# Short units' logits in a bank of their own, value products of two heads as column tiles, and moved steps at borders and in the state-space stage

## The chip, the core and the metric

The kernel runs on one core of one Trainium2 chip. The metric is device microseconds of one execution, as the median of three runs. The core's engines run side by side and meet only through semaphores: TensorE (PE in the profile, PEld for its weight loads), VectorE (DVE), ScalarE (ACT), GpSimd (POOL) and SyncE (SP), which here only issues loads. SBUF is the on-chip memory, PSUM the banks that TensorE writes.

## What is computed

Four layers on 256 tokens of width 1024, all float32: an "even" and an "odd" layer, then two hybrid layers. Each has a mixer and a gated convolution feed-forward part, each behind an RMS norm. The parts that the change touches, cut to what matters:

```python
# odd layer: dilated attention, 3 groups (window, dilation) x 4 heads of width 64
s = where(mask_g, q_g @ k_g.T, -inf)          # per head, 256 x 256, masks (128,1) (512,4) (2048,16)
m = max(s); p = exp(s - m); den = sum(p)
o = (p @ v_g) / den                           # lse = m + log(den)
out = sum_g softmax_g(lse) * o                # over the three groups
# hybrid layer: attention over the 64 best of 256 keys (8 heads of 128), beside a state-space scan
merged = sigmoid(g_attn) * (a @ w_proj_attn) + sigmoid(g_ssd) * (ssd @ w_proj_ssd)
# every norm
h = x * rsqrt(mean(x * x) + eps) * gain
```

Since the three groups share one softmax, the kernel masks the three groups' logits side by side in one row, takes one maximum, one exponential and one sum per row, and divides before the value product.

## The kernel before

Activations lie with channels on the 128 partitions and the 256 tokens along the free axis. Weights come as **slabs** of 2 halves, each 128 x 1024 (or 768, 512) float32. SP loads a slab into one of 3 slots (`w_raw`), ACT rounds it to fp32r (`w_hi`, line 1500), and POOL or DVE takes the remainder `w_lo = w_raw - w_hi` (`split_lo`, line 553). Each product is then three matmuls: hi by hi, hi by lo, lo by hi (`passes`, lines 784 to 786), or, in the feed-forward parts, a 512 wide one over the hi and lo operand side by side and a remainder (lines 805 and 809). ACT rounds 3 slabs ahead of the products, POOL and DVE split 2 slabs ahead: POOL half 0 and DVE half 1 in most stages. Results go to a ring of 4 PSUM banks `lin`; `logit`, `tr` and `stat` are PSUM too. Every engine works through its own program in the written order, so a wait holds up all that stands behind it on that engine.

**Dilated attention** (odd layer, once). 8 units u: head u // 2, token half t = u % 2. A short unit (t = 0) has 128 keys for each of 3 groups, a long one (t = 1) 256. The steps of a unit: `at_logits` on PE (line 1207, into `logit`), `at_mask` on DVE (scale and mask, line 2361, then the row maximum, line 2365), `at_exp` on ACT (line 1796), `at_probs` on DVE (reciprocal and scaling, lines 2373 and 2374), `at_transposes` on PE (line 1220, into `tr` and `stat`), `at_copy` on ACT (lines 1803 and 1805, to one of two buffers `pt1`), `at_values` on PE (line 1231: 3 or 6 matmuls of 64 output columns, into `lin`), `at_result` on ACT (line 1812). PE's program runs logits two units ahead of transposes, and values one behind; at_logits(u) waits until the mask of unit u - 1 has read the bank. Quarters of the first output slab (`late_part` of od_out[0]) stand between units. The four scans of the recurrence (line 2395), its gating (line 2399) and its rounding on ACT (line 1822) run at the same time. `v_copy(2)` (line 1789) empties the last slab of the values' projection, and PE waits for it (`stage_released`) before it goes on to unit 1.

**Borders.** A stage that adds to x (`residual` on ACT and POOL, `add_residual` on DVE) ends with four slabs j = 0 to 3, two channel chunks of x each. After each, ACT writes the gained x rounded and in float32 (line 1541), and its remainder `h_lo` is taken by POOL (chunks 0 to 3, line 562) or DVE (chunks 4 to 7). POOL's program: remainders of chunks 0, 1 after split j = 0, chunks 2, 3 after split j = 1, then split j = 2, a wait until DVE has taken all four of its remainders, and split j = 3. The first slabs of the next stage work on this not yet normalised h, and their results are scaled later; meanwhile `normalise` on DVE (lines 2023 to 2027) makes the normalised chunks in float32, ACT rounds them (`scaled`, line 1526) and POOL (4 chunks) and DVE (4 chunks) take the remainders `n_lo`. The up products of the two hybrid layers use them from slab 2 on; there PE waits first for all 8 rounded chunks, then chunk by chunk for the remainders. POOL splits both halves of the first slabs there, and `older_taps` on DVE (line 2143) runs the convolution.

**Hybrid layers** (twice). In the z stage, unit u of the sparse attention and two z slabs alternate; `by_token` (line 1348) transposes 4 chunks into `stat` and DVE copies them to SBUF (`stepped`, line 2599); the second transposes of a long unit (line 1374) need `stat` free. In the gates stage, DVE splits a slab's weights and then runs `ssd_out` (line 2650) for two chunks; PE's `group_cb` (line 1401) waits for it.

## Time and profile before

| what | value |
|---|---|
| median of 3 runs | 1689.92 us (1689.84 to 1690.18) |
| the profiled execution | 1691.72 us |
| its span | 1689.9 us |
| mean granted TensorE clock | 0.997 |
| PE busy | 1665.1 us, 99% |
| DVE busy | 1353.9 us, 80% |
| ACT busy | 1086.8 us, 64% |
| POOL busy | 754.0 us, 45% |
| DMA, mean of the 16 engines | about 50% |

"Busy" is the time in which at least one instruction of the engine was open. Matmuls overlap: a 256 wide fp32r matmul is open for 0.28 us, and the next one starts 0.12 us after it. A true float32 matmul is recorded as two instructions. "A <- B" means that A started when B had ended.

### The profile page before, as it was taken

The page shows a single profiled execution, that of the slowest core. Times are in us where ns is not written, and L with a number is a line of the kernel's source. Part 1 is how long each engine was busy: PE and PEld are TensorE (multiplying, and loading weights), DVE is VectorE, ACT ScalarE, POOL GpSimd, SP SyncE. Part 2 cuts the span into 40 slices and gives each one's busy share as a digit, 9 for nine tenths or more (in the row PEclk, how much of TensorE's full clock was granted, in tenths as well). Part 3 has the DMA queues.
Part 4 walks back from the last instruction along what each step waited for, and adds up shares of the span by engine and source line. Part 5 has one row for each costly group of instructions (what it writes and reads, how often), then busy time and mean ns, then how long its engine had stood idle before and what let it go on. Part 6 is the DMA issues. An engine that isn't in the chain of part 4 may idle for free. (4 is left out here: it accounts for less than half of the span.)

```text
span 1689.9 us, 28488 instructions
## 1 busy us (share of the span) xinstructions
PE 1665.1 (99%) x10944; PEld 1497.1 (89%) x10944; DVE 1353.9 (80%) x2174; ACT 1086.8 (64%) x1832; POOL 754.0 (45%) x454
## 2 busy tenths in 40 slices
PE   9999999999999999999999999999999999999997
PEld 8998889998888899999788988889999878888887
DVE  7978887494987878895996699778887699579795
ACT  7676576675775584776654676657467665378572
POOL 8631115962110367764554521048675465351113
PEclk9999999999999999999999999999999999999999
DMA  8545655541555555453345456556455335546552
GB/s 305 165 155 191 209 171 179 199 124 50 190 187 191 190 172 188 161 184 125 127 161 189 147 176 212 168 181 199 152 175 175 125 125 174 175 138 200 192 182 87
DMA packets 81239, 287.10 MB, mean 170 GB/s; under 512 B 9168, under 2 KB 9680, under 8 KB 80976
## 3 DMA queue, kind: packets, MB, share of 16 engines
q1 hardware_dynamic: 79776, 282.10, 50.4%
q10 hardware_dynamic: 1328, 3.18, 0.5%
q8 instruction: 87, 1.43, 0.3%
q14 instruction: 48, 0.39, 0.1%
HBM read 283.90 MB, written 1.05 MB: 169 GB/s over the span
## 5 line engine op out<-in xcount | busy, mean ns | idle before, releaser
L553 POOL TENSOR_TENSOR w_lo<-w_raw,w_hi 128x1024 fp32r<-128x1024 f32 (+2 forms) x239 | 570.2, 2405 | 308.7 <-ACT w_hi L1500 225.3
L1500 ACT ACTIVATE w_hi<-w_raw 128x1024 fp32r<-128x1024 f32 (+1 forms) x544 | 543.1, 1033 | 253.8 <-PE lin L786 162.7
L553 DVE TENSOR_TENSOR w_lo<-w_raw,w_hi 128x1024 fp32r<-128x1024 f32 (+1 forms) x305 | 456.7, 1502 | 31.0 <-ACT w_hi L1500 30.0
L784 PE MATMUL lin<-hid_pair,w_hi 128*128 128x256 f32 x1152 | 329.9, 286 | 1.8 <-POOL w_lo L553 1.7
L785 PE MATMUL lin<-hid_pair,w_hi 128*128 128x256 f32 x1152 | 326.1, 283 | 0.0
L786 PE MATMUL lin<-hid_pair,w_lo 128*128 128x256 f32 x1152 | 326.1, 283 | 0.0
L784 PEld LDWEIGHTS lin<-hid_pair,w_hi 128*128 128x128 f32 x1152 | 221.1, 192 | 6.3 <-issue 5.5
L785 PEld LDWEIGHTS lin<-hid_pair,w_hi 128*128 128x128 f32 x1152 | 221.2, 192 | 0.2
L786 PEld LDWEIGHTS lin<-hid_pair,w_lo 128*128 128x128 f32 x1152 | 221.2, 192 | 0.0
L562 POOL TENSOR_TENSOR hid_pair<-arena,hid_pair 128x256 fp32r<-128x256 f32 x64 | 53.3, 839 | 326.2 <-ACT std L1575 178.3
L805 PE MATMUL logit<-h_pair,w_hi 128*128 128x512 f32 x540 | 146.7, 392 | 0.0
L805 PE MATMUL lin<-h_pair,w_hi 128*128 128x512 f32 x540 | 136.2, 392 | 3.6 <-ACT h_pair L1526 1.7
L2143 DVE SCALAR_TENSOR_TENSOR acc<-arena,par,acc 128x254 f32<-128x254 f32 (+1 forms) x264 | 126.5, 521 | 7.6 <-ACT acc L1584 4.7
L805 PEld LDWEIGHTS lin<-h_pair,w_hi 128*128 128x128 f32 x540 | 101.0, 188 | 27.2 <-POOL h_pair L562 2.5
L805 PEld LDWEIGHTS logit<-h_pair,w_hi 128*128 128x128 f32 x540 | 97.1, 189 | 17.5
L784 PE MATMUL lin<-h_pair,w_hi 128*128 128x256 f32 x320 | 92.6, 289 | 2.1 <-POOL w_lo L553 1.4
L562 POOL TENSOR_TENSOR h_pair<-arena,h_pair 128x256 fp32r<-128x256 f32 x32 | 23.9, 757 | 152.1 <-ACT acc L1575 101.9
L785 PE MATMUL lin<-h_pair,w_hi 128*128 128x256 f32 x320 | 90.5, 283 | 0.0
L786 PE MATMUL lin<-h_pair,w_lo 128*128 128x256 f32 x320 | 90.5, 283 | 0.0
L805 PE MATMUL logit<-hid_pair,w_hi 128*128 128x512 f32 x324 | 89.1, 392 | 0.0
L784 PE MATMUL lin<-w_hi,hid_pair 128*128 128x512 f32 (+1 forms) x224 | 87.0, 388 | 0.0
L786 PE MATMUL lin<-w_hi,hid_pair 128*128 128x512 f32 (+1 forms) x224 | 84.0, 375 | 0.0
(407 smaller groups left out, 3581.6 us busy)
## 6 DMA issues: line engine op xcount, KB each, us to landing
w_raw<-in_upA SPq DMA_DIRECT2D x112, 512.0 KB, 4.5
w_raw<-in_upB SPq DMA_DIRECT2D x64, 512.0 KB, 4.6
w_raw<-in_xbc SPq DMA_DIRECT2D x48, 512.0 KB, 4.3
w_raw<-in_dnA SPq DMA_DIRECT2D x32, 512.0 KB, 4.5
w_raw<-in_dnB SPq DMA_DIRECT2D x32, 512.0 KB, 4.1
w_raw<-in_z SPq DMA_DIRECT2D x32, 512.0 KB, 4.4
w_raw<-in_gates SPq DMA_DIRECT2D x32, 512.0 KB, 4.4
w_raw<-in_ps SPq DMA_DIRECT2D x32, 512.0 KB, 4.0
```

Source lines behind the costliest of these rows:

```text
L553: eng.tensor_tensor(w_lo[slab.slot][:, half, part], w_raw[slab.slot][:, half, part], w_hi[slab.slot][:, half, part].bitcast(F32), ALU.subt ...
L562: return eng.tensor_tensor(lo, whole, hi.bitcast(F32), ALU.subtract)
L784: nc.tensor.matmul(out, lhs[0], rhs[0], start=first, stop=False)
L785: nc.tensor.matmul(out, lhs[0], rhs[1], start=False, stop=False)
L786: return nc.tensor.matmul(out, lhs[1], rhs[0], start=False, stop=last)
L805: return nc.tensor.matmul(outs[half], tile_of(slab, half, k)[0], pairs[k], start=(k == 0), stop=(half == 1 and k == last))
L1500: nc.scalar.activation(w_hi[slab.slot][:, half, part], w_raw[slab.slot][:, half, part], ACT.Copy)\
L2143: ins = stt(outs[i][:, d:T], ins_[i][:, 0:T - d], weight(taps - 1 - d, i), outs[i][:, d:T], ALU.mult, ALU.add)
```

## The change

It has seven parts.

1. **Logits.** Short units' logits go to the `lin` bank of od_out[1] (`at_early`), long units' stay in `logit`. at_logits(u) waits for the mask of unit u - 2, no longer of u - 1.
2. **Mask and maximum.** In the dilated and in the sparse attention, scaling, masking and the row extreme are one `tensor_tensor_reduce` (a negated sum and its minimum), which is emitted as the operation and a read of its accumulator. The exponential takes a scale of -1. The dilated one replaces two instructions by these two, the sparse one 4 + 1 by 4 x 2.
3. **Values.** Two heads' products with the same t form a pair and alternate matmul by matmul, one head in output columns 0 to 63, the other in 64 to 127, into one bank. They run after units 3, 4 and 7; `pt1` has 4 buffers instead of 2, and 4 result copies of 128 partitions replace 8 of 64.
4. **Border, POOL.** The split of j = 1 stands ahead of the remainders of chunks 0 and 1, and that of j = 2 ahead of those of chunks 2 and 3. The wait for DVE's last two remainders is gone; that for its first two stays.
5. **Normalised chunks.** POOL takes 3 remainders instead of 4, DVE 5; chunk 3 lies in `tr` in float32. The copy of the reciprocal root stands behind the remainders. In the hybrid layers' up products, PE waits for each rounded chunk as it comes to it. POOL holds back one split (slab 3, half 1) until the convolution taps of unit 0 are done.
6. **z stage.** The last by_token of u = 1 stands between the halves of its z slab.
7. **Gates stage.** At m = 3, DVE's weight split stands behind ssd_out.

PE in the dilated attention, before: unit 4's transposes, unit 3's values (6 matmuls), unit 7's logits. `lin` holds values here, `logit` logits.

```order
L1207 MATMUL logit<-arena 128x128 x3
L1220 MATMUL tr<-cst,arena 128x128 x3
L1231 MATMUL lin<-arena 64x128 x6
L1207 MATMUL logit<-arena 128x256 x3
L1220 MATMUL tr<-cst,arena 128x128 x4
L1220 MATMUL stat<-cst,arena 128x128 x2
L1231 MATMUL lin<-sq,arena 64x128 x3
```

The same place after:

```order
L1219 MATMUL lin<-arena 128x128 x3
L1232 MATMUL tr<-cst,arena 128x128 x3
L1246 MATMUL lin<-sq,arena 64x128 x12
L1219 MATMUL logit<-arena 128x256 x3
L1232 MATMUL tr<-cst,arena 128x128 x4
L1232 MATMUL stat<-cst,arena 128x128 x2
```

The 6 matmuls of unit 3 became 12 of units 1 and 3, the short unit's logits go to `lin`, and unit 4's values behind unit 5's transposes are gone from here.

POOL at the border before od_lru, before, with what each row waits for. `h_lo_v` counts DVE's remainders.

```order
L553 TENSOR_TENSOR w_lo<-w_raw,w_hi 128x768 [waits w_hi] x3
L562 TENSOR_TENSOR hid_pair<-arena,hid_pair 128x256 [waits h_f32,h_hi] x2
L553 TENSOR_TENSOR w_lo<-w_raw,w_hi 128x768 [waits w_hi]
L562 TENSOR_TENSOR hid_pair<-arena,hid_pair 128x256 [waits h_f32,h_hi] x2
L553 TENSOR_TENSOR w_lo<-w_raw,w_hi 128x1024 [waits w_hi]
L553 TENSOR_TENSOR w_lo<-w_raw,w_hi 128x1024 [waits w_hi,h_lo_v]
L553 TENSOR_TENSOR w_lo<-w_raw,w_hi 128x1024 [waits w_hi,w_lo1]
L553 TENSOR_TENSOR w_lo<-w_raw,w_hi 128x1024 [waits w_hi]
L562 TENSOR_TENSOR h_pair<-sq,h_pair 128x256 [waits n_f32,n_hi] x4
```

After:

```order
L565 TENSOR_TENSOR w_lo<-w_raw,w_hi 128x768 [waits w_hi] x4
L574 TENSOR_TENSOR hid_pair<-arena,hid_pair 128x256 [waits h_f32,h_hi] x2
L565 TENSOR_TENSOR w_lo<-w_raw,w_hi 128x1024 [waits w_hi]
L574 TENSOR_TENSOR hid_pair<-arena,hid_pair 128x256 [waits h_f32,h_hi] x2
L565 TENSOR_TENSOR w_lo<-w_raw,w_hi 128x1024 [waits w_hi,h_lo_v]
L565 TENSOR_TENSOR w_lo<-w_raw,w_hi 128x1024 [waits w_hi,w_lo1]
L565 TENSOR_TENSOR w_lo<-w_raw,w_hi 128x1024 [waits w_hi]
L574 TENSOR_TENSOR h_pair<-sq,h_pair 128x256 [waits n_f32,n_hi] x3
```

Each pair of remainders moved behind one more split, the last split's wait asks for two of DVE's remainders instead of four, and three normalised chunks are left to POOL.

The diff, cut to its core (declarations of the two semaphores that go are left out):

```diff
-            return sq[:, c, :] if c < DC // 2 else logit[:, c - DC // 2, :]
+            if c < NORM_POOL:
+                return sq[:, c, :]
+            return tr[:, T:2 * T] if c < DC // 2 else logit[:, c - DC // 2, :]
...
-        pt1 = (sqf[:, 0:6 * P], arena[:, 54 * T:57 * T])
+        pt1 = (arena[:, 54 * T:54 * T + 3 * P], sqf[:, 0:6 * P], arena[:, 54 * T + 3 * P:57 * T], sqf[:, 6 * P:12 * P])
...
         at_bank = [lin[slab_at("od_out", n).bank] for n in (2, 3)]
+        at_early = lin[slab_at("od_out", 1).bank][:, :, :].rearrange("p h t -> p (h t)")
+
+        def at_logit(t):
+
+            if t == 0:
+                return at_early[:, 0:DIL_G * P].rearrange("p (g k) -> p g k", g=DIL_G)
+            return logit[:, 0:DIL_G, :]
+
+        def at_pair_of(u):
+
+            return 2 * (u // 4) + u % 2
...
-                for c in range(DC // 2):
+                for c in range(NORM_POOL):
...
                 for k in range(COUNT[stage]):
                     j = k - (COUNT[stage] - 4)
-                    if j == 3 and n < 8:
-                        pool.wait_ge(s.h_lo_v, DC // 2 * n + 4)
                     split_lo(pool, slab_at(stage, k, l).ahead(SPLIT_AHEAD), 0)
-                    if j in (0, 1) and n < 8:
-                        norm_lo(n, (2 * j, 2 * j + 1))
+                    if j in (1, 2) and n < 8:
+                        norm_lo(n, (2 * j - 2, 2 * j - 1))
                     if j == 2 and n < 8:
                         pool.wait_ge(s.h_lo_v, DC // 2 * n + 2)
                     if j == 2 and n not in FOLDED:
...
                         for half in range(2):
+                            if k == 1 and half == 1:
+                                pool.wait_ge(s.ffn2_tap, 4 * l * FC + 4)
                             split_lo(pool, slab_at("upA" + sfx, k, l).ahead(SPLIT_AHEAD), half)
...
                 def wait_lo(k):
-                    half = DC // 2
-                    if k < half:
-                        pe.wait_ge(s.n_lo_p, half * number + k + 1)
+                    if k < NORM_POOL:
+                        pe.wait_ge(s.n_lo_p, NORM_POOL * number + k + 1)
                     else:
-                        pe.wait_ge(s.n_lo_v, half * number + k - half + 1)
+                        pe.wait_ge(s.n_lo_v, (DC - NORM_POOL) * number + k - NORM_POOL + 1)
...
                         def wait_chunk(c):
-                            if c == 0:
-                                wait_hi(KC - 1)
+                            wait_hi(c)
                             wait_lo(c)
...
             def at_logits(u):
                 head, t = u // 2, u % 2
                 lo = 64 * (head % 2)
-                if u >= 1:
-                    pe.wait_ge(s.at_masked, u)
+                if u == 0:
+                    slab_at("od_v", 0).wait_released(pe)
+                if u >= 2:
+                    pe.wait_ge(s.at_masked, u - 1)
                 for g in range(DIL_G):
                     c = (g * DIL_H + head) // 2
-                    mm = nc.tensor.matmul(logit[:, g, 0:(t + 1) * P], qn[lo:lo + 64, c, t * P:t * P + P],
+                    mm = nc.tensor.matmul(at_logit(t)[:, g, :], qn[lo:lo + 64, c, t * P:t * P + P],
                                           kn[lo:lo + 64, c, 0:(t + 1) * P], start=True, stop=True)
...
 
-            def at_values(u):
-                head, t = u // 2, u % 2
-                lo, nb = 64 * (head % 2), DIL_G * (t + 1)
-                pe.wait_ge(s.at_pt, u + 1)
-                if u >= 2:
-                    pe.wait_ge(s.at_out, u - 1)
+            def at_values(p):
+
+                units = (4 * (p // 2) + p % 2, 4 * (p // 2) + p % 2 + 2)
+                t, nb = p % 2, DIL_G * (p % 2 + 1)
+                pe.wait_ge(s.at_pt, units[1] + 1)
+                if p >= 2:
+                    pe.wait_ge(s.at_out, p - 1)
                 for b in range(nb):
-                    v_at = (b // (t + 1) * DIL_H + head) * DIL_D
-                    mm = nc.tensor.matmul(at_bank[u % 2][lo:lo + 64, 0, 0:P], vt[:, b % (t + 1), v_at:v_at + DIL_D],
-                                          pt1[u % 2][:, b * P:b * P + P], start=(b == 0), stop=(b == nb - 1))
+                    for u in units:
+                        head = u // 2
+                        lo, v_at = 64 * (head % 2), (b // (t + 1) * DIL_H + head) * DIL_D
+                        mm = nc.tensor.matmul(at_bank[p % 2][lo:lo + 64, 0, 0:P], vt[:, b % (t + 1), v_at:v_at + DIL_D],
+                                              pt1[u % 4][:, b * P:b * P + P], start=(b == 0), stop=(b == nb - 1))
                 mm.then_inc(s.at_pv, 1)
...
                     slab.wait_split(pe, half)
-            BESIDE = (2, 4, 6, 7)
+            BESIDE, VALUES_BEHIND = (2, 4, 6, 7), (3, 4, 7)
             for u in range(1, UNITS):
                 if u + 2 == 4:
                     slab_at("od_qk", 5).wait_released(pe)
@@ -1261,8 +1276,10 @@
                 if u + 2 < UNITS:
                     at_logits(u + 2)
                 at_transposes(u)
-                at_values(u - 1)
-            at_values(UNITS - 1)
+                if u in VALUES_BEHIND:
+                    at_values(VALUES_BEHIND.index(u))
+            at_values(3)
+            pe.wait_ge(s.at_masked, UNITS - 1)
...
+                    if u == 1:
+                        slab_products(slab_at("z", 2 * u + 1, l), operand, between=lambda: by_token(3))
+                    else:
+                        slab_products(slab_at("z", 2 * u + 1, l), operand)
+                        by_token(2 * u + 1)
 
                 pe.wait_ge(s.da_out, 4 * l + 4)
...
-                act.wait_ge(s.at_max, u + 1)
-                nc.scalar.activation(score[:, u % 2, 0:n], score[:, u % 2, 0:n], ACT.Exp,
+                act.wait_ge(s.at_masked, u + 1)
+                nc.scalar.activation(score[:, u % 2, 0:n], score[:, u % 2, 0:n], ACT.Exp, scale=-1.0,
                                      bias=small[:, 16 + u:17 + u], accum_out=small[:, 24 + u:25 + u]).then_inc(s.at_exp, 1)
 
...
                 n = DIL_G * (u % 2 + 1) * P
                 act.wait_ge(s.at_tr, u + 1)
+                if u >= 4:
+                    act.wait_ge(s.at_pv, at_pair_of(u - 4) + 1)
                 first = min(n, 4 * P)
-                ins = nc.scalar.activation(pt1[u % 2][:, 0:first], tr[:, 0:first], ACT.Copy)
+                ins = nc.scalar.activation(pt1[u % 4][:, 0:first], tr[:, 0:first], ACT.Copy)
                 if n > first:
-                    ins = nc.scalar.activation(pt1[u % 2][:, first:n], stat[:, T:T + n - first], ACT.Copy)
+                    ins = nc.scalar.activation(pt1[u % 4][:, first:n], stat[:, T:T + n - first], ACT.Copy)
                 ins.then_inc(s.at_pt, 1)
 
-            def at_result(u):
-                head, t = u // 2, u % 2
-                lo = 64 * (head % 2)
-                act.wait_ge(s.at_pv, u + 1)
-                nc.scalar.activation(acc[lo:lo + 64, 0, head // 2, t * P:t * P + P], at_bank[u % 2][lo:lo + 64, 0, 0:P],
-                                     ACT.Copy).then_inc(s.at_out, 1)
+            def at_result(p):
+                t = p % 2
+                act.wait_ge(s.at_pv, p + 1)
+                nc.scalar.activation(acc[:, 0, p // 2, t * P:t * P + P], at_bank[p % 2][:, 0, 0:P], ACT.Copy).then_inc(s.at_out, 1)
 
...
-                at_result(u - 1)
+                if u in (4, 5, 7):
+                    at_result((4, 5, 7).index(u))
                 if u + 2 < UNITS:
                     at_exp(u + 2)
-            at_result(UNITS - 1)
-            act.wait_ge(s.at_out, UNITS)
+            at_result(3)
+            act.wait_ge(s.at_out, 4)
             nc.scalar.activation(raw_set(1)[0][:, NC4:NC4 + 2, :], acc[:, 0, :, :], ACT.Copy).then_inc(s.att_hi, 1)
...
-                    act.wait_ge(s.da_max, 4 * l + u + 1)
+                    act.wait_ge(s.da_masked, 4 * l + u + 1)
                     for i in range(QPK):
-                        ins = nc.scalar.activation(da_score[u % 2][:, i, 0:n], da_score[u % 2][:, i, 0:n], ACT.Exp,
+                        ins = nc.scalar.activation(da_score[u % 2][:, i, 0:n], da_score[u % 2][:, i, 0:n], ACT.Exp, scale=-1.0,
...
+                for c in range(NORM_POOL, DC):
                     dve.wait_ge(s.n_hi, DC * number + (c | 1) + 1)
                     lo_part(nc.vector, lo[:, c, :], normed_f32(c), hi[:, c, :]).then_inc(s.n_lo_v, 1)
+                nc.vector.tensor_copy(std[:, 0, 0:T], rstd).then_inc(s.rstd_copied, 1)
                 dve.wait_ge(s.rstd_copied, number + 1)
-                dve.wait_ge(s.n_lo_v, DC // 2 * (number + 1))
+                dve.wait_ge(s.n_lo_v, (DC - NORM_POOL) * (number + 1))
 
...
-                stt(sc3, logit[:, 0:DIL_G, 0:n], DIL_D ** -0.5,
-                    dil[:, DIL_AT[t]:DIL_AT[t] + DIL_G * n].rearrange("p (g k) -> p g k", g=DIL_G), ALU.mult, ALU.add)\
-                    .then_inc(s.at_masked, 1)
-                dve.wait_ge(s.at_masked, u + 1)
-                nc.vector.tensor_reduce(small[:, 16 + u:17 + u], score[:, u % 2, 0:DIL_G * n], AX_X, ALU.max, negate=True)\
-                    .then_inc(s.at_max, 1)
+                nc.vector.tensor_tensor_reduce(
+                    sc3, at_logit(t),
+                    dil[:, DIL_AT[t]:DIL_AT[t] + DIL_G * n].rearrange("p (g k) -> p g k", g=DIL_G),
+                    -DIL_D ** -0.5, -TAKEN, ALU.add, ALU.min, small[:, 16 + u:17 + u]).then_inc(s.at_masked, 1)
 
...
-                        ins = stt(sc4[:, i, :], logit[:, i, 0:n], HD ** -0.5, sel[:, t, 0:n], ALU.mult, ALU.add)
+                        ins = nc.vector.tensor_tensor_reduce(sc4[:, i, :], logit[:, i, 0:n], sel[:, t, 0:n], -HD ** -0.5,
+                                                             -TAKEN, ALU.add, ALU.min, small[:, 16 + i:17 + i])
                     ins.then_inc(s.da_masked, 1)
-                    dve.wait_ge(s.da_masked, 4 * l + u + 1)
-                    nc.vector.tensor_reduce(small[:, 16:20], sc4, AX_X, ALU.max, negate=True).then_inc(s.da_max, 1)
...
                         ssd_seg(2 * m + 3)
-                    weights(slab_at("gates", m, l))
+                    if m != 3:
+                        weights(slab_at("gates", m, l))
                     ssd_out(2 * m, 2 * m)
                     ssd_out(2 * m + 1, 2 * m + 1)
+                    if m == 3:
+                        weights(slab_at("gates", m, l))
                     if m + 1 < XCH // 2:
```

## Rows read from the trace of the kernel before

**Rows 1.** The page, busy time of an engine, share of the span, instructions.

```profile
PE 1665.1 (99%) x10944; PEld 1497.1 (89%) x10944; DVE 1353.9 (80%) x2174; ACT 1086.8 (64%) x1832; POOL 754.0 (45%) x454
```

**Rows 2.** PE waits over the whole span: total us, times, longest.

```profile
PE lin L784 <- POOL w_lo L553: 3.2, 9, 0.6
...
PE lin L805 <- ACT h_pair L1526: 1.7, 2, 0.8
...
PE logit L809 <- DVE w_lo L553: 1.3, 2, 0.7
PE lin L805 <- DVE arena L2161: 1.1, 2, 0.6
PE tr L1401 <- DVE sq L2650: 0.9, 2, 0.4
PE lin L805 <- POOL h_pair L562: 0.8, 4, 0.2
...
PE stat L1374 <- DVE arena L2599: 0.7, 2, 0.3
PE lin L784 <- DVE h_pair L562: 0.6, 1, 0.6
```

**Rows 3.** Timeline of PE, dilated attention: start, us, work, [idle before <-releaser].

```profile
378.55 0.93 PE L1207 MATMUL logit<-arena 64*128 64x128 f32 x6
380.89 2.28 PE L1207 MATMUL logit<-arena 64*128 64x256 f32 x6 [1.41 <-DVE arena L2361]
...
399.98 0.87 PE L1231 MATMUL lin<-sq,arena 128*64 128x128 f32 x6
...
402.02 1.52 PE L1231 MATMUL lin<-arena 128*64 128x128 f32 x12
...
407.53 0.39 PE L784 MATMUL lin<-hid_pair,w_hi 128*128 128x256 f32 x1
```

**Rows 4.** Windows: PE, PEld, DVE, ACT, POOL busy, then PEclk, DMA.

```profile
380.00:390.00 10.00, 9.11 (x39) 7.07 (x40) 5.37 (x10) 5.78 (x13) 2.31 (x1) 0.66 0.20 69
382.00:384.00 2.00, 2.00 (x7) 1.25 (x7) 0.52 (x1) 1.12 (x3) 2.00 (x1) 0.50 0.00 0
```

**Rows 5.** PE group by form: shapes, records, shapes, count | busy us, mean ns | idle.

```profile
L1108 PE MATMUL tr<-arena 128*64 128x256 f32 x64 | 7.1, 380 | 0.0
```

**Rows 6.** Timeline of DVE, dilated attention.

```profile
371.45 4.03 DVE L2395 TENSOR_TENSOR_SCAN arena<-arena 128x256 f32<-128x256 f32 x4
...
377.89 1.22 DVE L2399 TENSOR_TENSOR arena<-arena 128x1024 f32<-128x1024 f32 x1
...
384.75 0.96 DVE L2361 SCALAR_TENSOR_TENSOR arena<-logit,arena 128x768 f32<-128x768 f32 x1 [2.23 <-PE stat L1220]
385.74 0.95 DVE L2365 TENSOR_REDUCE small<-arena 128x1 f32<-128x768 f32 x1
```

**Rows 7.** Timeline of ACT, dilated attention.

```profile
379.14 1.06 ACT L1822 ACTIVATE hid_pair<-arena 128x1024 fp32r<-128x1024 f32 x1 [0.63 <-DVE arena L2399]
380.11 0.58 ACT L1789 ACTIVATE arena<-lin 128x512 f32<-128x512 f32 x1
```

**Rows 8.** Timeline of POOL, border from the first feed-forward part to od_lru.

```profile
286.19 2.41 POOL L553 TENSOR_TENSOR w_lo<-w_raw,w_hi 128x1024 fp32r<-128x1024 f32 x1
294.29 2.40 POOL L553 TENSOR_TENSOR w_lo<-w_raw,w_hi 128x1024 fp32r<-128x1024 f32 x1 [5.69 <-DVE hid_pair L562]
```

**Rows 9.** Timeline of DVE, the same border.

```profile
287.14 2.54 DVE L553 TENSOR_TENSOR w_lo<-w_raw,w_hi 128x1024 fp32r<-128x1024 f32 x1
...
293.33 0.83 DVE L562 TENSOR_TENSOR hid_pair<-arena,hid_pair 128x256 fp32r<-128x256 f32 x2 [1.45 <-ACT arena L1541]
```

**Rows 10.** Timeline of POOL, opening of the up products, first hybrid layer.

```profile
966.90 2.81 POOL L562 TENSOR_TENSOR h_pair<-sq,h_pair 128x256 fp32r<-128x256 f32 x4
969.65 4.95 POOL L553 TENSOR_TENSOR w_lo<-w_raw,w_hi 128x1024 fp32r<-128x1024 f32 x2
```

**Rows 11.** Timeline of DVE, the same opening.

```profile
970.62 5.05 DVE L2143 SCALAR_TENSOR_TENSOR acc<-arena,par,acc 128x255 f32<-128x255 f32 x4 [1.16 <-ACT acc L1584]
```

7 lines of the change are left out of this document (1 added, 6 removed).

## The prediction

> **What bounds the kernel now.** I read the page's busy line first: PE is busy in 1665.1 us of the span's 1689.9 [rows 1], so PE sets the time in every stage, and only what shortens PE's own work or one of its idle gaps can count. Then I read PE's waits over the span, one line for each kind [rows 2]: they name gaps that the change touches, and each is small, 0.6 us or less in most places. Then the timeline of PE in the one stage whose PE work the change rewrites, dilated attention [rows 3], with windows of its clock [rows 4] and the DVE and ACT rows beside it [rows 6, 7]. Last, the POOL and DVE rows of one border and of one opening of the up products [rows 8 to 11], to see what ends the gaps there. Durations are of the profiled execution, 1691.72 us, 1.80 above the median of the runs; I sum against the former and take 1.80 off.
>
> **The dilated stage (parts 1 to 3).** It runs on PE from 378.55 to the start of od_out[1] at 407.53 [rows 3], 29.0 us. Four effects:
>
> *Values.* A short unit's product takes 0.80 us to the next instruction (0.87 in the row, its last matmul overlapping what follows) and a long one 1.45 (1.52) [rows 3]; four of each are 9.0 us. Afterwards two heads alternate as column tiles. The trace has that form elsewhere: the projections' transposed products of line 1108 also alternate two 64 wide column tiles, and their 64 records of 256 columns take 7.1 us, 0.111 each [rows 5]; the values' 12 records of only 128 columns take 1.52, 0.127 each [rows 3]. So an alternating record of twice the columns costs less than a lone one: two tiles do run side by side. At best a pair costs what a single unit costs: 2 x 0.80 + 2 x 1.45 = 4.5. If each of its 12 or 24 records, half as long as those of line 1108, costs 0.07 (a bit over half of 0.111), it is 2 x 0.98 + 2 x 1.8 = 5.6, with the drain behind the last. I take 4.7, near the best, as its records keep the columns and only share the array. Gain 4.3, bounds 3.4 and 4.5. ACT's four result copies in place of eight are no load.
>
> *The gap of 1.41 at 380.89.* PE's record blames the mask on DVE, but the same instruction waits for `v_copy(2)`, which ACT ends at 380.69 [rows 3, 7]. That copy stands behind the rounding of line 1822 (379.14, 1.06), which waited for the gating on DVE (377.89, 1.22), behind the scans [rows 6, 7]. The fused mask takes one long and one short unit's maximum out of DVE's program ahead of it: a long one's mask and maximum are 0.96 + 0.95 [rows 6]. Its replacement isn't in the trace. Near end: one pass like the mask, plus a short read of 0.1, so 1.0 for a long unit and 0.56 for a short one, 0.9 and 0.4 less than before. Far end: the pace of the scans, 4.03 / 4 = 1.0 for 256 elements with POOL beside it, which I scale down to 0.67 alone: 2.0 long, 1.05 short. I take the near end, since a plain sum feeding a minimum has no recurrence from element to element as a scan does. Then ACT is free 1.3 earlier and the gap shrinks to about 0.1: 1.3 gained.
>
> *The clock.* In the 10 us from 380 the granted clock is 0.66 on average, and 0.50, the lower of its two levels (1.2 GHz), in the window from 382 [rows 4]. (1 - 0.66) x 10 / 0.5 = 6.8 us at the lower level, right behind that gap. With the gap at 0.1 I expect it at the upper level: half of 6.8 is 3.4 gained, of which 0.1 to 0.5 comes back as waits of a faster PE. I take 3.3.
>
> *New waits.* I walked the three engines' programs of the stage with these durations (the walk of the kernel before puts od_out[1] at 407.52, against 407.53). After the change PE waits 0.4 for the gated output's remainder, 0.2 and 0.7 for the probabilities of units 3 and 7, 0.4 and 0.3 for the copies of units 5 and 7: 2.0 in all, against 0.7 before outside the gap, so about 1.4 lost. The lower number of buffers waited for (two units apart) costs PE nothing in the walk.
>
> Sum: -4.3 - 1.3 - 3.3 + 1.4 = **-7.5**. With the far price of the fused mask the walk gives -3.5 instead, since DVE then holds PE up in every unit.
>
> The sparse attention's masks (4 fused instructions and 4 reads for 4 + 1) lie on DVE under PE work that doesn't wait for them in any line of [rows 2]. At the near price they take no longer than before; at the far price a unit's masks take some us more, under the two or more slabs of each unit. Nought; if that cover were gone, the far price would show in full.
>
> **Borders (part 4, and the order in part 5).** PE waits 3.2 us for POOL's remainders of weights in 9 places and 0.6 for a remainder of DVE's [rows 2]. At the border shown POOL stands idle for 5.69 us, waiting for DVE's last remainder (chunk 7, 293.33 to 294.16), and only then takes the split of j = 3, 294.29 to 296.69 [rows 8, 9]: PE, which waits 0.6 for it, needs it at about 296.2. Afterwards that split asks for DVE's first two only, which are done by 290.5 (DVE's split of 287.14 ends at 289.68, two remainders take at most 0.83 [rows 9]), so it ends some 3 us earlier and the wait goes. Of the 9 waits one of 0.2 is not at such a border. Further, DVE's split takes 2.54 beside POOL's 2.41 [rows 8, 9], where a DVE pass of that size without POOL beside it takes 1.22 [rows 6]; the new order spreads them. Waits for remainders on POOL (0.5 in 2 places) should go with the chunk moved to DVE. Gain 3.0 + 0.6 + 0.3 = **-3.9**. POOL's own remainders each stand behind one more split of 2.4 us; PE comes to them one slab later at the earliest, some 3 us, so they may give back up to 0.3 a border: bounds 2 and 4.5.
>
> **Up products of the hybrid layers (part 5).** In each of the two layers PE waits 0.83 for all rounded chunks, about 0.2 twice for POOL's remainders, 0.55 for line 2161 and 0.65 for a weight remainder: the lines of 1.7, 0.8, 1.1 and 1.3 in [rows 2], 4.9 together. POOL takes 2.81 for four remainders, then 4.95 for two splits, and DVE's four taps, begun at 970.62, take 5.05 beside them [rows 10, 11]. Waiting chunk by chunk removes most of the 0.83, a remainder less on POOL 0.7 of its delay, and the held-back split leaves the taps alone, which then end earlier than the 5.05 by up to 3 us (2.54 against 1.22 above shows what POOL beside it costs a DVE pass). Behind the held-back split PE may wait for its remainder instead, but there are two slabs between. **-4.5**; bounds 2 (only the chunk-wise wait) and 6 (unattributed gaps beside the named ones too).
>
> **z and gates stages (parts 6 and 7).** PE's second transposes wait 0.7 in two places for `stepped` on DVE; a half slab put between hides that. group_cb waits 0.9 in two places for ssd_out, which now stands ahead of a DVE split of some 1.2 to 2.5; that split's own slab is a slab away. 1.6 in all [rows 2]: **-1.5**, bounds 0 and 2.
>
> **Sum.** -7.5 - 3.9 - 4.5 - 1.5 = -17.4: 1691.7 - 17.4 = 1674.3 for the profiled execution, **1672.5 us** as the median.
>
> **Rivals.**
>
> *The clock falls in the stage all the same* (0.18). The new waits of 0.2 to 0.7 come close upon each other, and the one fall that the stage shows came behind 1.41 of idle; an opening gap still of 0.5 or more could start it. For: 0.4 for the remainder stands right at the start. Against: gaps of 0.6 at borders leave the mean clock near 1. Cost: the 3.3 less the waits that a slow PE hides, 2.9: about 1675.5.
>
> *The fused mask runs at the pace of the scans* (0.08). Cost 4.0 in the dilated stage: 1676.5.
>
> *Column tiles don't overlap* (0.05). Each pair then takes twice a unit, 1.6 and 2.9; the change would not do what part 3 says, and the walk gives -3.7 for the stage: 1676.3. The rows speak against it: 0.111 for 256 columns against 0.127 for 128 [rows 3, 5].
>
> The Trainium skill, TensorE: Matmul & The Clock Gate, Part 3, The mechanism, states that a weight load overlaps matmuls in flight only when its row group differs. Both heads' tiles use all 128 rows and differ in columns alone, so by it the weight loads would not hide and this rival would hold. By that rule the trace does not agree: line 1108's tiles share their rows too.
>
> *Half of the borders' and openings' gain stays away* (0.10): the wait passes to the next late thing, ACT's rounding of the slab or its copies. 4 less: 1676.5.
>
> *Slower* (0.02). POOL's split of j = 3, freed of its wait, could be running when ACT delivers chunks 6 and 7 (DVE takes them from 293.33), and slow DVE's two remainders, 0.83 together [rows 9], up to its own length: 2.4 us a border, with PE, which has no wait as long as that to hide it, waiting for chunk 7's. Each mixer and feed-forward part but the last ends in a border: 7 x 2.4 = 16.8 and the borders' 3.9 lost: 1672.5 + 16.8 + 3.9, about 1693.2. It decides if POOL's split of j = 3 ends later than 293.3. From DVE's first two remainders at 290.5, or 1.2 earlier with DVE's split less slowed, plus 2.4, it ends at 291.7 to 292.9: a margin of 0.4 to 1.6 against it, and where they meet only the overlap counts.
>
> *Nothing changes* (0.02), if some stage's loads set the time: DMA is at about half of its time.
>
> **How the numbers follow.** The main case holds 0.55, with its own range 1669.5 to 1675. The rivals lie at 1675.5 to 1676.5, or 1680 for two of them at once. With all gains at their upper bounds (-7.9, -4.5, -6, -2) it is 1669.5, a little less if gaps go that no row names: low 1668.5. High 1680.5 takes in two rivals together. A measurement here can tell about 0.2% (3.4 us) from no change, so only the slower rival and the nothing case lie outside faster: 0.95 faster, 0.03 same, 0.02 slower.
>
> **What would show it.** Right: the dilated stage takes 21.5 us instead of 29.0 from unit 2's logits to od_out[1]; the clock stays at 1.00 there; a pair's 24 records last about 1.6 us; the fused mask of 768 elements about 1.0; the 1.41 is gone; PE's lines for w_lo, line 1526's h_pair and line 2161 in the list of waits sink to under 1.5 us together; PE busy falls by about 4.3 plus 3.4. Wrong: a clock of 0.5 in any window of the stage; fused masks of 2 us; a pair of 2.9 us; POOL's last split of a border touching DVE's remainders, seen as rows over 0.45 each; new lines of waits for POOL's h_lo or for ACT's w_hi.

## The result

| kernel | median us | ratio to before, 95% interval |
|---|---|---|
| before, in the same series | 1690.05 (1689.84 to 1693.20, 4 runs) | |
| changed | 1679.77 (1677.63 to 1681.97, 4 runs) | 0.9935 (0.9917 to 0.9953) |
| changed, measured once more | 1681.87 (1677.35 to 1683.72, 4 runs) | 0.9939 (0.9919 to 0.9959) |

The change makes the kernel 0.6% faster, 10.3 us in the first series and 8.6 in the second. The direction was forecast, the size was not: 10.3 us instead of 17.4. The first median lies in the range at its upper end, the second 1.4 us above its end of 1680.5. The changed kernel's times spread over 6.4 us, where those of the best kernel below spread over 0.9; why is the main thing that the runs showed.

The profiled execution took 1679.26 us (span 1677.5), against 1691.72 for the one before. The page's busy line, against [rows 1]: PE busy fell by 10.8 us, DVE by 20.

```profile
PE 1654.3 (99%) x10944; PEld 1491.6 (89%) x10944; DVE 1333.7 (80%) x2204; ACT 1086.0 (65%) x1828; POOL 752.4 (45%) x448
```

PE's waits over the span, against [rows 2] (total us, times, longest). The code has moved by 12 lines or more: L817 and L821 are the lines 805 and 809 of before, L796 is 784, L1421 is 1401, L1391 is 1374, L2182 is 2161.

```profile
PE lin L817 <- DVE arena L2182: 2.8, 2, 1.4
...
PE lin L796 <- DVE hid_pair L574: 1.7, 1, 1.7
PE logit L821 <- DVE w_lo L565: 1.3, 2, 0.7
...
PE tr L1421 <- DVE sq L2668: 0.8, 2, 0.4
...
PE stat L1391 <- DVE arena L2617: 0.7, 2, 0.3
```

The waits of L784 for `w_lo` are gone from the list, as forecast, and those of L805 for the rounded `h_pair` of L1526 fell from 1.7 to 0.2. But those for L2161, now L2182, rose from 1.1 to 2.8, so the three lines that were to sink to under 1.5 together stand at 3.0. One of 1.69 for `hid_pair` is new; the one of L784 for DVE's `h_pair` remainder, 0.6, stayed and is 0.8; and the waits of parts 6 and 7 stand as they stood, 0.7 in two places and 0.8 for 0.9.

The timeline of PE in the dilated stage, against [rows 3]:

```profile
378.58 0.93 PE L1219 MATMUL lin<-arena 64*128 64x128 f32 x6
379.74 1.53 PE L1219 MATMUL logit<-arena 64*128 64x256 f32 x6 [0.22 <-issue]
...
383.76 0.35 PE L796 MATMUL lin<-hid_pair,w_hi 128*128 128x256 f32 x1 [1.69 <-DVE hid_pair L574]
...
388.36 0.88 PE L1246 MATMUL lin<-arena 128*64 128x128 f32 x12
...
391.40 1.53 PE L1246 MATMUL lin<-sq,arena 128*64 128x128 f32 x24
...
401.61 0.39 PE L796 MATMUL lin<-hid_pair,w_hi 128*128 128x256 f32 x1
```

The stage takes 23.03 us (378.58 to 401.61) instead of 28.98. The gap of 1.41 at the long unit's logits shrank to 0.22, a pair of short units' values takes 0.88 and a pair of long ones' 1.53, exactly what a single unit's took. New is the 1.69 at 383.76, where the gated output's remainder was forecast at 0.4.

Here is where the 12.4 us between the two traces went, read from the starts of the same matmuls of PE in both. The last column is the kernel with part 4 alone (second experiment).

| stretch | forecast | changed | part 4 alone |
|---|---|---|---|
| start to the border before od_lru | 0 | +1.5 | +0.2 |
| six borders that moved | -3.9 | -5.3 | -4.5 |
| dilated stage | -7.5 | -5.95 | +0.1 |
| two openings of up products, to the next norm | -4.5 | -2.7 | -3.1 |
| z and gates stages | -1.5 | 0.0 | 0.0 |
| sum | -17.4 | -12.4 | -7.3 |

The changed kernel's +1.5 at the start belongs to that one execution: the nine profiles below of it, or of kernels built on it, are 1.1 to 2.1 us ahead of it when they reach the dilated stage. The rows show what it was, DVE first and then POOL:

```profile
12.55 4.58 DVE L574 TENSOR_TENSOR w_lo<-w_raw,w_hi 128x512 fp32r<-128x512 f32 x2
```

```profile
11.55 2.23 POOL L656 TENSOR_TENSOR sq<-sq 128x512 f32<-128x512 f32 x1 [2.47 <-ACT sq L1529]
14.13 2.45 POOL L565 TENSOR_TENSOR w_lo<-w_raw,w_hi 128x1024 fp32r<-128x1024 f32 x1 [0.35 <-ACT w_hi L1520]
```

The two halves of `w_lo` take 1.28 together in the trace of before, and took 4.58 here beside POOL's two instructions; PE waited 1.10 for them. More on that below.

### The profile page after: what moved, and what is told of

It is laid out like the page before. It is cut to its first block and busy times, and to the rows that moved or that the text cites. A ratio compares the mean times of both kernels' runs of the same rounds, so it can differ in the third digit from the quotient of the medians.

```text
span 1677.5 us, 28519 instructions
## 1 busy us (share of the span) xinstructions
PE 1654.3 (99%) x10944; PEld 1491.6 (89%) x10944; DVE 1333.7 (80%) x2204; ACT 1086.0 (65%) x1828; POOL 752.4 (45%) x448
## 3 DMA queue, kind: packets, MB, share of 16 engines
q8 instruction: 87, 1.43, 0.3%
## 5 line engine op out<-in xcount | busy, mean ns | idle before, releaser
L565 DVE TENSOR_TENSOR w_lo<-w_raw,w_hi 128x1024 fp32r<-128x1024 f32 (+1 forms) x305 | 444.7, 1462 | 30.7 <-ACT w_hi L1520 29.7
L796 PE MATMUL lin<-hid_pair,w_hi 128*128 128x256 f32 x1152 | 329.9, 286 | 1.7 <-DVE hid_pair L574 1.7
L796 PEld LDWEIGHTS lin<-hid_pair,w_hi 128*128 128x128 f32 x1152 | 220.9, 192 | 4.1 <-issue 3.3
L817 PE MATMUL logit<-h_pair,w_hi 128*128 128x512 f32 x540 | 146.7, 392 | 0.0
L817 PE MATMUL lin<-h_pair,w_hi 128*128 128x512 f32 x540 | 135.0, 390 | 3.2 <-DVE arena L2182 2.8
L2164 DVE SCALAR_TENSOR_TENSOR acc<-arena,par,acc 128x254 f32<-128x254 f32 (+1 forms) x264 | 119.8, 495 | 7.5 <-ACT acc L1604 4.6
L817 PEld LDWEIGHTS lin<-h_pair,w_hi 128*128 128x128 f32 x540 | 101.1, 188 | 25.4 <-DVE arena L2182 3.7
L817 PEld LDWEIGHTS logit<-h_pair,w_hi 128*128 128x128 f32 x540 | 97.2, 189 | 17.4
L796 PE MATMUL lin<-h_pair,w_hi 128*128 128x256 f32 x320 | 92.9, 290 | 0.9 <-DVE h_pair L574 0.8
L817 PE MATMUL logit<-hid_pair,w_hi 128*128 128x512 f32 x324 | 89.1, 392 | 0.0
L796 PE MATMUL lin<-w_hi,hid_pair 128*128 128x512 f32 (+1 forms) x224 | 87.0, 388 | 0.0
L797 PE MATMUL lin<-w_lo,hid_pair 128*128 128x512 f32 (+1 forms) x224 | 84.0, 375 | 0.0
```

Source lines behind the costliest of these rows:

```text
L565: eng.tensor_tensor(w_lo[slab.slot][:, half, part], w_raw[slab.slot][:, half, part], w_hi[slab.slot][:, half, part].bitcast(F32), ALU.subt ...
L796: nc.tensor.matmul(out, lhs[0], rhs[0], start=first, stop=False)
L797: nc.tensor.matmul(out, lhs[0], rhs[1], start=False, stop=False)
L817: return nc.tensor.matmul(outs[half], tile_of(slab, half, k)[0], pairs[k], start=(k == 0), stop=(half == 1 and k == last))
L2164: ins = stt(outs[i][:, d:T], ins_[i][:, 0:T - d], weight(taps - 1 - d, i), outs[i][:, d:T], ALU.mult, ALU.add)
```

## The experiments

Each kernel is built on the changed kernel or on the one before; the stage's length is from unit 2's logits to the start of od_out[1] on PE (378.55 to 407.53 before, 28.98 us). "Low" is how long the granted clock stood at 0.50 in the stage, worked out from windows.

| run | median us (range, runs) | stage us | low us |
|---|---|---|---|
| before | 1690.1 to 1690.5 in each series | 28.98 | 6.8 |
| changed | 1679.77 (1677.63 to 1681.97, 4) | 23.03 | 0 |
| e1 parts 1 to 3 alone | 1690.25 (1684.11 to 1691.96, 10) | 29.17 | 13.7 |
| e2 part 4 alone | 1684.18 (1682.46 to 1685.33, 5) | 29.06 | 6.8 |
| e3 values single | 1679.56 (1) | 25.48 | 0 |
| e4 two masks | 1681.68 (1) | 27.46 | 3.4 + 3.4 |
| e5 changed, again | 1681.87 (1677.35 to 1683.72, 4) | 27.58 | 10.2 |
| e6 remainder first | 1676.37 (1675.86 to 1677.34, 4) | 21.69 | 0 |
| e7 split on DVE | 1678.59 (1) | 27.58 | 10.2 |
| e8 steps at the waits | 1680.49 (1) | 27.49 | 10.2 |
| e9 parts 1 to 3, remainder first | 1684.42 (1684.32 to 1684.70, 6) | 21.69 | 0 |
| e10 not held | 1679.94 (1) | 27.47 | 10.2 |
| e11 four on POOL | 1683.05 (1) | 27.58 | 10.2 |
| e12 all together | 1670.22 (1669.80 to 1670.66, 4) | 21.69 | 0 |

### e1 and e2: the two large parts apart

e1 is the kernel before with parts 1 to 3, e2 with part 4 and nothing else:

```diff
-                    if j == 3 and n < 8:
-                        pool.wait_ge(s.h_lo_v, DC // 2 * n + 4)
...
-                    if j in (0, 1) and n < 8:
-                        norm_lo(n, (2 * j, 2 * j + 1))
+                    if j in (1, 2) and n < 8:
+                        norm_lo(n, (2 * j - 2, 2 * j - 1))
```

> The kernel before with parts 1 to 3 alone (logits' bank, fused masks in both attentions, value pairs); no border or opening is touched. Theory: these parts are worth what the dilated stage shows in the changed kernel, 29.0 to 23.0 us from unit 2's logits to od_out[1], so 1690.05 - 6.0 = 1684 us; the gated output's remainder on DVE again takes about 2.9 us instead of 1.2, beside POOL's split. Rival: the stage also profits from the reordered border ahead of it and alone brings 4 us or less (1686), or, as the prediction had it, 7.5 (1682.5).

> The kernel before with part 4 alone (POOL's order at the borders and the two waits for DVE's remainders). Theory: all of the borders' gain read from the changed kernel's trace, some 6 us, comes from this part, so about 1684 us, and each border's wait for POOL's remainder of weights is gone from PE. The prediction's own figure, 3.9, would give 1686.2. Rival: a good share of it comes from part 5's third normalised chunk on DVE, and part 4 alone brings 3 us or less (1687 or more).

e1 gave nothing in most of its executions: ratio 0.9992 (0.998 to 1.0003). Neither theory nor rivals had that. Its profile shows all the pieces of the gain, and a stage that is as long as before. Windows of e1 (PE, PEld, DVE, ACT, POOL busy, then PEclk, DMA):

```profile
384.00:388.00 4.00, 4.00 (x18) 3.12 (x18) 1.93 (x8) 1.91 (x4) 0.00 (x0) 0.62 0.32 115
388.00:392.00 4.00, 4.00 (x19) 2.83 (x19) 0.97 (x2) 1.09 (x4) 0.00 (x0) 0.50 0.02 4
392.00:396.00 4.00, 4.00 (x21) 3.22 (x18) 0.79 (x4) 1.12 (x3) 0.00 (x0) 0.50 0.00 0
396.00:400.00 4.00, 4.00 (x32) 3.38 (x32) 1.84 (x6) 1.37 (x4) 0.00 (x0) 0.68 0.00 0
```

(0.38 + 0.50 + 0.50 + 0.32) x 4 us / 0.5 = 13.6 us at the lower level, 1.2 GHz, which costs PE 6.8 us. Of these 6.1 show in the stage's length (29.17 against the changed kernel's 23.03), and that is all that the stage had gained. Of the ten timed executions of e1 two came out at 1684.1 and 1685.7, with a mean clock of 0.998; the rest have 0.994 to 0.997 and 1688.9 or more.

e2 came out as the theory said, 1684.18, ratio 0.9962 (0.9948 to 0.9976). POOL and DVE at the border before od_lru, against [rows 8, 9]:

```profile
290.19 2.41 POOL L553 TENSOR_TENSOR w_lo<-w_raw,w_hi 128x1024 fp32r<-128x1024 f32 x1 [3.57 <-DVE hid_pair L562]
```

```profile
287.36 1.22 DVE L553 TENSOR_TENSOR w_lo<-w_raw,w_hi 128x1024 fp32r<-128x1024 f32 x1
...
293.20 0.83 DVE L562 TENSOR_TENSOR hid_pair<-arena,hid_pair 128x256 fp32r<-128x256 f32 x2 [1.45 <-ACT arena L1539]
```

POOL's split of j = 3 starts at 290.19, 4.1 us earlier than before, and ends at 292.60, before DVE takes chunks 6 and 7 at 293.20. That is 0.6 us of margin against the slower rival; the prediction had 0.4 to 1.6. DVE's split takes 1.22 instead of 2.54, as it no longer lies beside POOL's.

### e3 and e4: the pairs and the fused mask taken back

e3 puts the values back unit by unit, e4 makes mask and maximum two instructions again:

```diff
-                if u in VALUES_BEHIND:
-                    at_values(VALUES_BEHIND.index(u))
-            at_values(3)
+                at_values(u - 1)
+            at_values(UNITS - 1)
```

> The changed kernel with the values as before, unit by unit behind the next unit's transposes (6 or 12 records each, one column tile), four copy buffers and the other parts kept. Theory: a pair costs what a single unit costs (0.88 and 1.53 us in the changed kernel's trace), so the stage grows by the four products that come back, 2 x 0.80 + 2 x 1.45 = 4.5 us, less what PE's waits there (2.0 + 1.3 us) hide of it: 2.5 to 4.5 longer, 25.5 to 27.5 us. Rival: the pairs save little because PE then waits for ACT and DVE anyway: under 1.5 us longer.

> The changed kernel with the dilated attention's mask and maximum as two instructions again (0.5 + 0.55 and 0.96 + 0.95 us); the sparse attention keeps the fused form. Theory of the prediction: a gap of about 1.4 us comes back at the end of the values' projection, the granted clock falls to 0.5 behind it for some 7 us, and the stage takes 23.0 + 1.3 + 3.3 or more, 27.5 us. Rival, since the changed kernel had 1.69 us of idle in the stage at a clock of 1.00: the gap doesn't bring the clock down, and the stage takes 24 to 25.5 us at a clock of 1.00.

e3: 25.48 against 23.03, both without a fall of the clock: the pairs are worth 2.45 us, the low end of what was expected. They take 4.5 us of work from PE, as the rows of the changed kernel say, but 2 us of that PE spends waiting. 0.8 of these lie at the gated output's remainder, where e3's first value product fills a part of the gap (0.89 for 1.69), and the rest at the units' probabilities and copies. With that gap gone (e6, below) the pairs should be worth more; no run has both.

e4: 27.46 was the theory's number, though not its sum. The clock fell twice, for some 3.4 us each, and not once for 7, so it took 3.4 of the 4.4 us, which leaves 1.0. That isn't the fused mask's worth alone: in e4 DVE starts the gated output's remainder ahead of POOL's split again (379.32 against 379.91), and the gap of 1.69 isn't there. Against the kernels below without that gap and without a fall (21.69), the two instructions cost some 2.4 us. PE's waits in the stage and two windows:

```profile
PE tr L1233 <- DVE arena L2396: 2.9, 3, 1.7
...
PE logit L1220 <- DVE arena L2383: 1.4, 1, 1.4
```

```profile
380.00:384.00 4.00, 4.00 (x19) 3.22 (x18) 2.01 (x3) 2.03 (x5) 2.21 (x1) 0.59 0.13 44
400.00:404.00 4.00, 4.00 (x39) 3.68 (x37) 0.00 (x0) 1.15 (x3) 0.00 (x0) 0.57 0.02 4
```

The first fall lies behind the gap of 1.43 that came back, the second (0.57 in the window from 400) behind the longest of the waits of L1233, 1.74 us, which ended at 399.44.

### e5 and e6: the same kernel again, and DVE's remainder ahead of POOL's split

e5 is the changed kernel unaltered. e6 adds one wait on POOL:

```diff
                     j = k - (COUNT[stage] - 4)
+                    if stage == "od_out" and k == 0:
+                        pool.wait_ge(s.lru_y_lo, 1)
                     split_lo(pool, slab_at(stage, k, l).ahead(SPLIT_AHEAD), 0)
```

> The changed kernel once more, unaltered, to see how the granted clock spreads over its executions. Theory: the clock falls in the dilated stage in some executions and not in others, for lengths that differ (the kernel before 7 us, the dilated parts alone 13 us, the changed kernel 0 in its profile), so times spread from 1677.5 (mean clock 0.999) to 1685 or so (0.995), some 4 us for each 0.0025 of mean clock. Rival: the changed kernel keeps the clock up because its stage has fewer gaps; then all of its times lie within 1.5 us of each other beside the start's 1.5 us.

> The changed kernel, with POOL's split beside the dilated attention's start held until DVE has taken the gated output's remainder. Theory: DVE's remainder of 128x1024 took 2.85 us because POOL's split began 0.04 us earlier; held back, it takes 1.22 and PE's wait for it falls from 1.69 to about 0.1, the stage from 23.0 to 21.5 us where the clock stays up; POOL's split is not needed for another 10 us. The clock falls less often. Rival: the unit chain (masks, exponentials, copies) takes the time back later in the stage, 22.5 us or more.

In e5 the clock fell for 10.2 us in the stage, from the same gap of 1.69 us on, and the stage took 27.58 us:

```profile
380.00:384.00 4.00, 2.31 (x13) 1.88 (x12) 3.27 (x5) 2.15 (x6) 0.81 (x1) 0.79 0.40 130
384.00:388.00 4.00, 4.00 (x13) 3.02 (x13) 1.26 (x4) 1.20 (x3) 0.00 (x0) 0.50 0.00 1
388.00:392.00 4.00, 4.00 (x22) 2.75 (x21) 1.46 (x4) 1.59 (x3) 0.00 (x0) 0.50 0.02 4
392.00:396.00 4.00, 4.00 (x40) 3.40 (x40) 1.43 (x5) 1.68 (x6) 0.00 (x0) 0.93 0.00 0
```

The same windows of the changed kernel's profile have 1.00 in all four; one of them:

```profile
380.00:384.00 4.00, 2.31 (x14) 1.66 (x14) 3.96 (x6) 2.85 (x6) 1.82 (x1) 1.00 0.08 26
```

So that profile, with its 23.03, showed the rarer case. What made the gap is in the changed kernel's rows of DVE and POOL:

```profile
379.55 0.56 DVE L2382 CUSTOM_DVE_ANT_0 arena<-lin,arena 128x384 f32<-128x384 f32 x1 [1.60 <-PE lin L1219]
...
380.76 2.85 DVE L574 TENSOR_TENSOR hid_pair<-arena,hid_pair 128x1024 fp32r<-128x1024 f32 x1
383.54 0.94 DVE L2382 CUSTOM_DVE_ANT_0 arena<-logit,arena 128x768 f32<-128x768 f32 x1
```

```profile
380.72 1.82 POOL L565 TENSOR_TENSOR w_lo<-w_raw,w_hi 128x768 fp32r<-128x768 f32 x1 [4.12 <-ACT w_hi L1520]
```

DVE's remainder of 128x1024 needs 1.22 us ([rows 6] has a pass of that size), and took 2.85: POOL's split began 0.04 us ahead of it and ran until 382.54, its usual 1.82, and DVE ended 1.07 after that. So they did not share at half pace: the later one stood still until the first had ended, or nearly so. The Trainium skill says so (SBUF — State Buffer, Who interferes with whom): the port pair that DVE and GpSimd share is an exclusive lock, and a DVE instruction with two SBUF inputs contends with a GpSimd one that reads SBUF; the trace agrees. In the kernel before, DVE was 0.58 us ahead at this place, took its 1.22, and POOL's split was the one that took longer:

```profile
381.30 1.22 DVE L562 TENSOR_TENSOR hid_pair<-arena,hid_pair 128x1024 fp32r<-128x1024 f32 x1
```

```profile
381.88 2.31 POOL L553 TENSOR_TENSOR w_lo<-w_raw,w_hi 128x768 fp32r<-128x768 f32 x1 [4.76 <-ACT w_hi L1500]
```

In e6, DVE, POOL and PE:

```profile
379.32 1.22 DVE L574 TENSOR_TENSOR hid_pair<-arena,hid_pair 128x1024 fp32r<-128x1024 f32 x1
```

```profile
380.62 1.83 POOL L565 TENSOR_TENSOR w_lo<-w_raw,w_hi 128x768 fp32r<-128x768 f32 x1 [5.48 <-DVE hid_pair L574]
```

```profile
380.69 0.36 PE L798 MATMUL lin<-hid_pair,w_hi 128*128 128x256 f32 x1
```

1.22 us again, no wait at PE's product, 21.69 us for the stage, and no low clock in it. The four executions lie within 1.5 us, 1675.86 to 1677.34, where those of e5 spread over 6.4. Held against e5, one wait on an idle engine is worth 5.5 us: 1.3 for the gap, and the rest for a clock that doesn't fall.

### e9: is it the gap that lets the clock fall?

e9 is e1 with the same wait on POOL.

> The dilated parts alone on the kernel before (as in the run of parts 1 to 3 alone, 1690.25 us), and POOL's split held until DVE has taken the gated output's remainder. Theory: the 1.69 us gap at that remainder is what let the granted clock fall there for 13.7 us; without it the clock stays at 1.00 in the stage, the stage takes 21.5 us, and the kernel 1690.3 less 7.5, 1682 to 1683 us in most executions. Rival: the clock falls for other reasons (many short gaps in a stage of small matmuls), in about as many executions as without the hold: median above 1687.

1684.42, ratio 0.9964 (0.9951 to 0.9976), six executions within 0.4 us, where e1 had 1690.25 and a spread of 7.9. The stage is 21.69 us long. That carries the theory of the gap; the median is 1.4 above what was expected of it, on which more below. Over all profiles:

| longest gap of PE ahead of or in the stage's first half | profiles | with a fall of the clock in the stage |
|---|---|---|
| 1.4 us at the long unit's logits (before, e2, e4) | 3 | 3 |
| 1.69 us at the gated output (changed, e1, e5, e7, e8, e10, e11) | 7 | 6 |
| 0.89 us there (e3) | 1 | 0 |
| 0.23 us (e6, e9, e12) | 3 | 0 |

How long it stays down differs from execution to execution, and once in seven the gap of 1.69 brought no fall; no run here shows what sets either. Outside this stage (and the end of the kernel, where every profile has some 6 to 8 us of low clock) there is one fall more, in e9: 3.4 us from 1497 on, behind the gaps of 0.83 and twice 0.19 of the second opening of up products. It cost nothing at the next norm, since PE had waits behind it to lose.

### e7, e10 and e11: the openings of the up products

The rows of the changed kernel there, DVE, POOL and PE, against [rows 10, 11]:

```profile
962.25 1.67 DVE L2164 SCALAR_TENSOR_TENSOR acc<-arena,par,acc 128x255 f32<-128x255 f32 x4 [1.16 <-ACT acc L1604]
964.01 2.66 DVE L2215 TENSOR_TENSOR arena<-std,acc 128x256 f32<-128x256 f32 x1
```

```profile
964.00 2.39 POOL L565 TENSOR_TENSOR w_lo<-w_raw,w_hi 128x1024 fp32r<-128x1024 f32 x1 [2.56 <-DVE acc L2164]
```

```profile
971.54 1.67 PE L817 MATMUL lin<-h_pair,w_hi 128*128 128x512 f32 x6 [1.40 <-DVE arena L2182]
```

The four taps need 1.67 us now instead of 5.05. But POOL, which had been held back until their end, starts its split at that very moment, and the multiply behind them (0.43 alone) takes 2.66. PE then waits 1.40 instead of 0.55. e10 takes the hold away, e7 gives the split to DVE, and e11 sets `NORM_POOL = 4`:

```diff
-                            if k == 1 and half == 1:
-                                pool.wait_ge(s.ffn2_tap, 4 * l * FC + 4)
...
+                            if c == 0:
+                                dve.wait_ge(s.w_lo[1], slab.number + SPLIT_AHEAD + 1)
+                                split_lo(dve, slab.ahead(SPLIT_AHEAD + 1), 1)
                             dve.wait_ge(s.ffn2_t0, l * FC + c + 1)
```

(e10 has the first piece alone; e7 has the second, and POOL leaves that split out.)

> The changed kernel, with the held-back split (slab 3, half 1 of the up products of the hybrid layers) on DVE, in its idle 1.16 us before the taps of unit 0, instead of on POOL behind the taps. Theory: POOL's split is what holds the multiply behind the taps for 2.66 instead of 0.43 us; without it unit 1 starts some 2 us earlier on DVE, and PE's wait for the third unit's sums, 1.40 in each layer, goes: 2.5 to 3 us in all. Rival: that wait is the end of a chain of fixed length (product, first tap on ACT, taps, multiply) and falls by 0.3 us at most in each layer.

> The changed kernel, with POOL's split of slab 3, half 1, not held back but run right behind the one before it, as in the kernel before; the rest of part 5 stays. Theory: holding it only moved the block from the taps (5.05 us instead of 1.67) to the multiply behind them (2.66 instead of 0.43), so without it the opening of each hybrid layer's up products is 0.3 to 1.0 us slower, PE's wait for the third unit's sums about 2 us instead of 1.40. Rival: it did nothing or harm, and the opening is as fast or faster.

> The changed kernel with four normalised chunks' remainders on POOL again and four on DVE (as before the change); order, waits and the held-back split stay. Theory: POOL's fourth remainder takes 0.7 us there, and PE waits for it at the openings: 0.2 to 0.7 us more at each of the two up openings, and 0.2 us more at the first feed-forward part's; 1 us in all. Rival: since PE waits for DVE's chain a moment later anyway, the fourth chunk is worth nothing there: under 0.3 us from the border to the second slab pair's end.

Their times can't be compared as such, since the clock fell for 10.2 us in all three; the same matmuls of PE can. From the opening's first product to the next norm, against the changed kernel: e10 -0.89 and -0.90 in the two layers, e7 -2.05 and -2.06, e11 -0.15 and -0.16. DVE and POOL of e10:

```profile
964.71 3.02 DVE L2162 SCALAR_TENSOR_TENSOR acc<-arena,par,acc 128x255 f32<-128x255 f32 x4 [1.17 <-ACT acc L1602]
967.82 0.42 DVE L2213 TENSOR_TENSOR arena<-std,acc 128x256 f32<-128x256 f32 x1
```

```profile
961.48 4.78 POOL L565 TENSOR_TENSOR w_lo<-w_raw,w_hi 128x1024 fp32r<-128x1024 f32 x2
```

I had expected e10's openings to be slower, and they were faster: with the split right behind the others, the taps lose 1.35 us to it (3.02 for 1.67), the multiply nothing. Holding the split back cost 0.9 us a layer. In e7, DVE takes it in the 1.16 us in which it waits for ACT:

```profile
964.44 1.51 DVE L565 TENSOR_TENSOR w_lo<-w_raw,w_hi 128x1024 fp32r<-128x1024 f32 x1
...
967.62 0.42 DVE L2218 TENSOR_TENSOR arena<-std,acc 128x256 f32<-128x256 f32 x1
967.96 0.68 DVE L2190 TENSOR_TENSOR arena<-lin,std 128x512 f32<-128x512 f32 x1
```

The multiply is at 0.42, unit 1 follows at once, and PE's waits for L2182 are gone. The theory of e7 holds, its rival falls. e11's rival holds for the openings; the chunk moved to DVE is worth 0.45 and 0.29 us elsewhere, at the borders to the hybrid layers' mixers.

### e8 and e12: parts 6 and 7, and all together

e8 moves the steps of parts 6 and 7 at u = 2 and m = 1 too:

```diff
-                    if u == 1:
+                    if u in (1, 2):
...
-                    if m != 3:
+                    if m not in (1, 3):
```

> The changed kernel, with the z stage's transposes between the halves at u = 2 as well, and the gates' split behind the output sums at m = 1 as well as m = 3. Theory: parts 6 and 7 gained nothing because they moved the steps at u = 1 and m = 3, while the two waits on PE (0.35 and 0.42 in each layer) stand behind u = 2 and m = 1; moved there, both go: 1.5 us less between the same places of the program. Rival: the waits are set by POOL's split beside DVE or by the copies themselves and stay, or turn up as waits for weight remainders: under 0.5 us.

The z stage's wait went, with 0.58 us in each layer, so part 6's step had been moved in the wrong unit. The gates' wait stayed. DVE, POOL and PE there:

```profile
835.56 3.03 DVE L565 TENSOR_TENSOR w_lo<-w_raw,w_hi 128x1024 fp32r<-128x1024 f32 x1
838.51 0.47 DVE L2668 SCALAR_TENSOR_TENSOR sq<-arena,par,tr 128x256 f32<-128x256 f32 x1
```

```profile
835.12 2.39 POOL L565 TENSOR_TENSOR w_lo<-w_raw,w_hi 128x1024 fp32r<-128x1024 f32 x1
```

```profile
839.04 0.70 PE L1421 MATMUL tr<-arena 128*128 128x256 f32 x2 [0.42 <-DVE sq L2668]
```

DVE's split takes 3.03 us beside POOL's, the sums stand behind it. I had the place wrong a second time: `group_cb` runs ahead of m = 0 and behind m = 1, 3 and 5; of its four rows in a layer, some 16 us apart, only the last has a wait. That is m = 5. e12 moves the split there (and not at m = 3) and takes e6, e7 and the z step in.

> The changed kernel with all that the runs pointed to: POOL's split held behind the gated output's remainder, slab 3's half 1 split on DVE before the taps in both hybrid layers, the z stage's transposes between the halves at u = 2 too, and the gates' split behind the output sums at m = 5 (where the one wait of 0.42 stands) instead of m = 3. Theory: from 1676.4 (remainder first) another 3.5 to 4.2 for the openings, 1.0 for z and 0.8 for gates: 1670.5 to 1671.5 us, clock 0.998 or more. Rival: the openings' gain was hidden by the low clock in its one run and is 2 us or less, and the split moved at m = 5 brings a wait for its remainder: 1673 or more.

1670.22, ratio 0.9881 (0.9866 to 0.9896), all four executions within 0.9 us. Against e6's trace: z -0.6 in each layer, the gates' m = 5 -0.43 and -0.41, the openings -2.06 each. Of its waits on PE the longest are these:

```profile
PE logit L1084 <- POOL arena L728: 2.1, 1, 2.1
PE tr L1234 <- DVE arena L2398: 1.0, 2, 0.8
PE lin L798 <- DVE h_pair L574: 0.8, 1, 0.8
```

## The prediction, step by step

**What bounds the kernel** held: PE sets the time everywhere, and where a run took a wait away, PE's later matmuls started earlier by it, or by more (see the borders).

**Values**: the price of a pair was right at its near end (0.88 and 1.53), so the term of -4.3 holds as PE's work. Its worth at the stage's end is 2.45 (e3), since new waits come with it, which the sum has as a term of their own, and 0.8 of them is the gap at the remainder.

**The gap of 1.41 and the fused mask**: right. The gap went (0.22 left), the fused mask takes 0.96 and 0.56 (its near price 1.0 and 0.56), and neither of the rivals on its pace and on serial tiles came about. The Trainium skill's rule that a weight load overlaps matmuls in flight only when its row group differs (TensorE: Matmul & The Clock Gate, Part 3, The mechanism), weighed in the prediction, did not hold for pairs that differ in columns alone: 24 records took 1.53 us, what 12 had taken.

**New waits**: here the working failed. The walk gave DVE's remainder 1.22 us and PE a wait of 0.4; it was 2.85 and 1.69. The walk had PE, DVE and ACT in it and not POOL, though the prediction used POOL's effect on a DVE pass (2.54 for 1.22) two paragraphs later. Before the change DVE started that remainder first. The change brought DVE's program and POOL's split to the same moment, and POOL won by 0.04 us. Those 1.3 us are most of the difference between -7.5 and the -5.95 of the profile: with POOL out of the way the stage took 21.69 us (e6, e9, e12), a gain of 7.3, near the 7.5 of the sum.

**The clock**: the step "with the gap at 0.1 I expect it at the upper level" failed, because the gap was replaced by a longer one. The rival that the clock falls all the same had 0.18; it is what 6 of the 7 profiles with the gap of 1.69 show. Its price, 2.9, was taken from the 6.8 us of before; it is 4.5 (27.5 against 23.0), or 6.1 in e1. In the changed kernel's usual execution the whole stage brings about 1.4 us.

**Borders**: -3.9 was too low, with -5.3 in the trace. The mechanism was right: e2 shows the split 4.1 us earlier and DVE's split at 1.22. The mis-sized term is PE's waits. The sum took the idle time that the list names, but a wait costs PE more than that, since a matmul is open for 0.28 us and the next one, if nothing holds it, starts 0.12 after it. PE of the kernel before, at the wait of this border:

```profile
295.63 0.59 PE L942 MATMUL stat<-sq,cst 128*128 128x256 f32 x2
296.83 0.36 PE L784 MATMUL lin<-hid_pair,w_hi 128*128 128x256 f32 x1 [0.61 <-POOL w_lo L553]
```

For 0.61 of idle time the matmuls behind it start 0.85 us earlier in e2; the other five borders' largest waits, 0.59, 0.60, 0.60, 0.15 and 0.14, gave 0.82, 0.84, 0.84, 0.38 and 0.37. Against that, the 0.6 for a remainder of DVE's, counted as gained, stayed (0.8 in the changed kernel and in e12).

**Openings**: -4.5 was too high. "The held-back split leaves the taps alone" was right, and what stood behind the taps was not looked at: that cost 1.8, and without the hold (e10) the trace has -4.45. That this is the forecast number is luck, as the prediction gave all of it to part 5. Part 4 alone brings -3.1 there (e2): with it PE's waits of 0.2 for POOL's remainders go. Part 5 without the hold adds 1.4; in e10 and e11 the wait of 0.83 for the rounded chunks is gone, in e2 it is 0.77. No run has the chunk-wise wait alone.

**z and gates**: -1.5 and got 0. The waits' sizes were right, their places were not looked up: the list of waits names a line, and the line runs in several units.

**The two executions**: I took 1.80 us off for the profiled execution's distance from the median. Between the profiled executions e9 is 7.3 us shorter than before, between the medians 5.7. The profiled execution of before may have had a longer low clock than most, and then its 3.4 us of it can't be gained in full from the median. That fits, but the timed runs have no windows, so it is argued and not shown.

The sum of what failed: 1.5 for the start's chance, 1.5 for the dilated stage at full clock and 4.5 more where it falls, 1.8 and 1.5 for openings and steps, less 1.4 for the borders. That the first median still lies in the range owes something to the range's width: its upper end was made for two rivals at once, and what filled it was one of them at a higher price together with openings and steps that gave less.

## What to carry to other kernels

Before adding or removing work on DVE, lay POOL's timeline beside it: here POOL's splits and DVE's passes with two inputs in SBUF excluded each other (2.85 us for 1.22, 2.66 for 0.43), and a shift of half a microsecond decided which one waited. Put such a pair in an order by a wait where the loser is on the path, or give the instruction to the engine that is idle there. And look up in which iteration a wait stands before moving a step for it; of seven profiles with the same gap of 1.69 us on PE, one lost nothing by the clock behind it, five lost half of 10.2 us and one half of 13.7, that is three to four times the gap, so such a gap is worth closing first.

## What the runs showed of the hardware

- POOL's split of 128x768 and DVE's of 128x1024, started 0.04 us apart: 1.82 and 2.85 us; one behind the other: 1.83 and 1.22. A multiply of 128x256 beside POOL's split, started 0.01 us after it: 2.66 for 0.43. Where DVE was first (by 0.58 us, before) it took its 1.22 and POOL 2.31.
- The granted clock fell to 0.50 behind gaps of PE of 1.4 to 1.7 us in 9 of 10 profiles, and stayed there for 3.4 to 13.7 us in different executions; never in the stage in the four whose longest gap was 0.9 us or less (once elsewhere behind one of 0.83).
- Two float32 products of 128 columns on two column tiles, alternating, take the time of one: 1.53 us for 24 records against 1.52 for 12.
- `tensor_tensor_reduce` runs at the pace of the plain masked pass (0.96 us for 768 elements, 0.56 for 384) with 0.08 us for reading its accumulator.
